# Mixture-of-experts backbone step on one core: the loop over overflow units on TensorE reshaped from two passes of five into one pass and nine, with the counts for unused passes added by VectorE or ScalarE

## The reference, cut to what matters

```python
g_idx = jnp.argmax(g_logits, axis=-1)                 # one of 4 groups
top_v, top_i = lax.top_k(e_logits, TOP_K)             # 2 of the group's 4 experts
top_w = jax.nn.softmax(top_v, axis=-1) * g_w
expert_id = g_idx[:, None] * EXPERTS_PER_GROUP + top_i
combine = jnp.sum(one_hot(expert_id, N_EXPERTS) * top_w[..., None], axis=1)
hidden = silu(einsum('nd,edf->nef', x, w_gate)) * einsum('nd,edf->nef', x, w_up)
y = einsum('nef,efd->nd', hidden * combine[:, :, None], w_down)
```

## Time and profile before

| | |
|---|---|
| time, median of 3 runs | 1340.03 us (1337.36 to 1342.93) |
| span of the profiled execution | 1339.8 us |
| PE busy (matmul) | 1237.9 us, 92% |
| PE weight loads busy | 685.1 us, 51% |
| DVE / ACT / POOL busy | 519.8 / 299.0 / 134.4 us |
| moved from and to device memory | 346.14 MB, mean 258 GB/s |
| granted TensorE clock, mean | 0.984 of full speed |

### The profile page before, as it was taken

The page is one execution under the profiler, slowest core; times in us unless marked ns, Lnnn a source line. Parts: engine busy times, 40 slices in busy tenths (PEclk is TensorE's granted clock), DMA queues, the critical chain, the costliest instruction groups (busy, mean ns, idle before and its releaser), DMA issues. The chain is left out here.

```text
span 1339.8 us, 14616 instructions
## 1 busy us (share of the span) xinstructions
PE 1237.9 (92%) x5692; PEld 685.1 (51%) x5692; DVE 519.8 (39%) x1021; ACT 299.0 (22%) x713; POOL 134.4 (10%) x142
## 2 busy tenths in 40 slices
PE   5999989999998988788999999999999989999897
PEld 2543356445543334244767766776676454453332
DVE  1376666043100002544543646546565561000035
ACT  2123245042111110105121222211223241111112
POOL 0079900000000010001101000000000000000010
PEclk8999999999999999898999999999999999999999
DMA  9859995465999995531232321322234849999995
GB/s 383 338 195 381 373 418 241 187 253 226 403 422 424 426 427 238 247 126 44 99 125 72 141 79 71 134 83 113 83 110 167 378 180 393 424 427 424 426 425 227
DMA packets 35958, 346.14 MB, mean 258 GB/s; under 512 B 3984, under 2 KB 9360, under 8 KB 16528
## 3 DMA queue, kind: packets, MB, share of 16 engines
q1 hardware_dynamic: 23328, 315.37, 57.9%
q0 software_dynamic: 5040, 18.35, 3.4%
q10 hardware_dynamic: 7488, 11.01, 2.3%
HBM read 326.10 MB, written 18.61 MB: 257 GB/s over the span
## 5 line engine op out<-in xcount | busy, mean ns | idle before, releaser
L656 PE MATMUL PS<-ring,hT 128*128 128x512 f32 x432 | 190.5, 595 | 0.0
L872 PE MATMUL PS<-ring,hT 128*64 128x512 f32 x736 | 169.1, 607 | 18.5 <-issue 10.9
L656 PEld LDWEIGHTS PS<-ring,hT 128*128 128x128 f32 x432 | 81.3, 191 | 98.5 <-issue 97.7
L872 PEld LDWEIGHTS PS<-ring,hT 128*64 128x64 f32 x736 | 59.6, 140 | 124.0 <-issue 119.8
L1077 PE MATMUL PS<-ring 128*128 128x256 f32 x480 | 108.7, 379 | 1.2 <-ACT ring L1525 1.2
L1077 PEld LDWEIGHTS PS<-ring 128*128 128x128 f32 x480 | 91.1, 190 | 14.0 <-issue 1.6
L2086 DVE TENSOR_TENSOR area<-area,PS 128x512 f32<-128x512 f32 x16 | 11.0, 688 | 222.0 <-PE PS L872 222.0
L892 PE MATMUL PS<-ring,area 128*64 128x512 f32 x400 | 91.2, 605 | 4.6 <-DMA ring<-moe_w_down 2.4
L1058 PE MATMUL PS<-ring,area 128*128 128x512 f32 x192 | 83.8, 593 | 3.8 <-ACT area L1613 3.8
L1077 PE MATMUL PS<-ring,hT 128*128 128x256 f32 x360 | 82.6, 379 | 0.0
L872 PE MATMUL PS<-area,hT 128*64 128x512 f32 x272 | 69.0, 618 | 12.3 <-issue 12.3
(11 more groups left out here) (308 smaller groups left out, 1507.7 us busy)
## 6 DMA issues: line engine op xcount, KB each, us to landing
ring<-moe_w_down SPq DMA_DIRECT2D x25, 2048.0 KB, 19.4
ring<-mod_w SPq DMA_DIRECT2D x24, 2048.0 KB, 11.3
ring<-moe_w_up SPq DMA_DIRECT2D x24, 2048.0 KB, 14.5
ring<-moe_w_gate SPq DMA_DIRECT2D x22, 2048.0 KB, 14.8
ring<-in_w SPq DMA_DIRECT2D x20, 2048.0 KB, 7.9
area<-moe_w_up SPq DMA_DIRECT2D x8, 2048.0 KB, 15.3
area<-moe_w_gate SPq DMA_DIRECT2D x8, 2048.0 KB, 14.7
ring<-out_w SPq DMA_DIRECT2D x7, 2048.0 KB, 8.8
```

The costliest lines, as they stand in the source:

```text
L656: mm = pe.matmul(out, lhs(k), rhs(k), start=k == 0, stop=k == KD - 1)
L872: mm = pe.matmul(PS[64 * e:64 * e + 64, j, :], gT[:, 4 * half + k, 64 * e:64 * e + 64], w[e][k], start=half == 0 and k == 0, stop=half == ...
```

## The change

On TensorE the loops change from two groups of five to a first pass of one unit and a second pass of nine: the inner loop runs `v * (OVS - 2) + 1` times, which is one for v = 0 and nine for v = 1. The outer `If` has no `Else` any more. Where a pair has exactly one unit, the counts of the nine others are added to `ov_pe` by another engine, ACT for pairs 0 to 5 and DVE for pairs 6 and 7, beside the counts that it adds there already.

```diff
-OVG = 5
...
-                        with pe.Fori(0, OVS // OVG) as v:
-                            with pe.If(n > v * (OVG * OVC) + CAP):
-                                with pe.Fori(0, OVG) as u:
-                                    with pe.If(n > v * (OVG * OVC) + u * OVC + CAP):
-                                        unit(p, v * (OVG * da) + u * da + a, v * (OVG * db) + u * db + b,
-                                             v * (OVG * dc) + u * dc + c, v * OVG + u + e, W)
+                        with pe.Fori(0, 2) as v:
+                            with pe.If(n > v * OVC + CAP):
+                                with pe.Fori(0, v * (OVS - 2) + 1) as u:
+                                    with pe.If(n > v * OVC + u * OVC + CAP):
+                                        unit(p, v * da + u * da + a, v * db + u * db + b, v * dc + u * dc + c, v + u + e, W)
                                     with pe.Else():
-                                        pe.wait_ge(ov_pe, v * (OVG * da) + u * da + a)
+                                        pe.wait_ge(ov_pe, v * da + u * da + a)
                                         pe.sem_inc(ov_pe, da)
                                     pe.nop()
-                            with pe.Else():
-                                pe.wait_ge(ov_pe, v * (OVG * da) + a)
-                                pe.sem_inc(ov_pe, OVG * da)
                             pe.nop()
...
                             act.wait_ge(ov_act, b + db)
                             act.sem_inc(ov_act, db * (OVS - 1))
                             if not direct:
+                                act.sem_inc(ov_pe, da * (OVS - 1))
                                 act.wait_ge(ov_stored, 32 * o + 48)
...
                             dve.wait_ge(ov_dve, c + dc)
                             dve.sem_inc(ov_dve, dc * (OVS - 1))
+                            if direct:
+                                dve.sem_inc(ov_pe, da * (OVS - 1))
                             dve.wait_ge(ov_picks, e + 2)
```

## The result

The changed kernel takes 1333.57 us (median of 5 runs, 1332.43 to 1338.18), the kernel before 1342.93 beside it: ratio 0.994, 95% interval 0.9921 to 0.9958. Run again among the experiments it gave 0.9944 (0.9929 to 0.9959), so some 8 us are gone. The forecast was 1332.7, range 1329.5 to 1338.5. The profiled executions, 1339.8 and 1330.6 us, differ by 9.2.

What follows compares the result with a forecast made beforehand. PE, busy 92% of the span, was taken to bound the kernel, its sequencer walking through empty loop code behind pair 6's unit. 1340.0 - 5.2 - 3.0 + 0.3 + 0.6 = 1332.7 us, range 1329.5 to 1338.5.

Steps and rivals of the forecast that it cites:

- The passes that go: Behind pair 6's unit in layer 0: four skipped passes of 1.17 us go, 4.7 us; with the tail, idle shrinks 5.2 us.
- Where PE starts again: Pair 7's first matmul in layer 0 moves from 547.2 to 542.0, 5.2 us, bounds 5.0 and 5.5.
- The clock: Pair 7's first sixteen matmuls behind the gap no longer run slowly: 3.0 us gained, bounds 0 and 3.0.
- the nearer row: Behind pair 6: 0.3 us idle taken as like the unit's pauses (clock held), not the 2.42 us stop (0.56).
- the clock falls all the same: Rival behind pair 6: sparse matmuls and short gap still lower the clock, only 5.2 us gained, 1335.7; chance 0.12.
- the gap only changes its name: Rival at pair 7's start: another wait or the new arithmetic keeps PE idle some 4 us, 1338 to 1340; chance 0.08.
- Pair 7: Behind pair 7's unit, layer 0: no gain, DVE is last and 5.6 us idle stays; slow spell behind costs 0.3 more.
- DVE in addition: One more semaphore instruction on DVE, 0.1 us with its gap, fits in 0.24 us free: costs nothing.
- Where the code comes to lie: Line 1015's short-way branches: moved code may turn them long or short, 2.3 us each; 0.6 us lost taken.
- The rivals built on the branches: One to three short branches turn long, 1334.4 to 1339.0, chance 0.14; all four, 1341.3 or 1344.3, chance 0.06.

Runs made afterwards that it cites:

- an idle time made in another way: Changed kernel plus 80 (or 24) already satisfied waits before pair 7's gate sweep in layer 0; ratio to the kernel before 0.9971 (24 waits: 0.9943).
- the execution with the 40 waits: Kernel before plus 40 satisfied waits in pair 0's jumped-over overflow code, never executed, so later TensorE code lies 40 instructions further; ratio 0.9996.
- the stop by hand: Kernel before plus 56 satisfied waits in front of pair 5's gate sweep in layer 0; ratio 0.9989.
- the ten skips: Kernel before with one group of ten units instead of two of five (OVG 10), nine skips instead of four; 1348.49 us, ratio 1.0056.
- TensorE adding the counts: Changed kernel's loops, but TensorE adds the nine counts in an outer Else, ScalarE's and VectorE's additions removed; ratio to the kernel before 0.9954.
- the filled gap: Kernel before, skips left, plus six idle-filling matmuls behind pair 6's unit in layer 0; ratio 0.9972.
- all gaps filled: Changed kernel plus six filling matmuls behind pair 7's unit and two ahead of ten short ways; ratio to the kernel before 0.9939.

## Why the prediction was right

**The passes that go** were right, place and size: 5.31 us against 5.2, with no skip left. Five more of them made the idle time 3.9 us longer (4.5 expected), and an idle time made in another way cost its length at the place too. (Of the taken branches in the earlier trace rows one took 176 and one 323 ns, so 215 to 229 does not hold for all; the passes' own were 215 to 226, and the sum stands.)

**Where PE starts again:** the forecast start was 542.0, the trace has 539.44; 2.44 of the difference is the lead that came from before pair 6. The exit compared with a register cost nothing that can be seen: the sequencer is ready 0.2 us behind the unit's end.

**The clock** was right, 2.93 against 3.0, and the choice of the nearer row holds: at this place 0.20, 0.91 and 1.78 us leave it up, 4.61 and 5.51 bring it down. The rival "the clock falls all the same" is out, and so is "the gap only changes its name": nothing else was late. That the size fits so well is in part luck. Behind nearly the same gap the sixteen matmuls lost 2.80 us in the execution with the 40 waits (6.45 against 3.65) and only 1.56 in that with the stop by hand, and behind the 9.38 us of the ten skips 1.39. Between 1.9 and 2.7 us the length of an idle time alone does not tell whether the clock falls. PE's timelines of the stop by hand, of the changed kernel and of TensorE adding the counts:

```profile
546.82 5.21 PE L872 MATMUL PS<-ring,hT 128*64 128x512 f32 x16 [5.46 <-PEq L1040]
```

```profile
484.48 5.35 PE L871 MATMUL PS<-area,hT 128*64 128x512 f32 x16 [1.97 <-issue]
```

```profile
493.53 3.66 PE L871 MATMUL PS<-ring,hT 128*64 128x512 f32 x16 [2.68 <-DMA ring<-moe_w_up]
```

Behind 1.97 us the granted clock was 0.68 (484.4 to 489.8 us), behind 2.68 it was 1.00 (493.5 to 497.1). What decides there is not shown.

**Pair 7** gained nothing, as said; the slow spell behind it has 0.4 us more PE work in it (from 596.29 to 600.87 against 606.98 to 611.16), so 0.2 us lost against 0.3.

**DVE in addition** cost nothing: the semaphore at 541.7 stands in time that DVE had free, for behind its sums DVE still waits 1.34 us for PE.

**Where the code comes to lie** was mis-sized. The step priced a branch that turns long at 2.3 us and took a quarter of one. It also counted ten of the fourteen branches as showing: nine do, and the tenth stop is the one at 1269.63 in the middle of a sweep. One short branch did turn long, and PE stopped 2.63 us, but in layer 0 the price was nothing: the wait for weights absorbs it (the stop in pair 5 shows that). In layer 1 the price of a stop was not shown: the changed kernel stands 11.2 us for "issue" there instead of 14.0, without the stop in the sweep, and takes no less time for it. The rivals built on the branches were wrong in price for layer 0, not only in count.

The Trainium skill ("Runtime: NRT & Kernel Launch", "Instruction fetch mechanics") is borne out in that jumps to far code stop the engine. The same section of the Trainium skill calls the crossing of a fetched block mostly hidden. That agrees with most packets, for of the 70 that queue 8 brings in the kernel before, 55 come without a jump of line 1015 and without a stop for "issue" of over 0.4 us; the stops of 2.87 and 2.13 us in the middle of a sweep, each with a packet landing in it, are not hidden.

Against the sum: 5.3 + 2.9 + 2.4 (pair 6's earlier end) - 0.2 make 10.4, and 9.2 are measured in the traces. The 1.2 between are lost in layer 1, where some spells of low clock and waits moved. In none of the thirteen profiled executions does a unit run in layer 1, and from its first transposes to the end they take from 732.8 us (the kernel before) to 738.5 (ten skips), so a loss of 1 or 2 us there can't be put down to the change. The mechanism was right at the place; that the total came so near is in part luck, since 2.4 us came that were not forecast and 1.2 went. In layer 1's pair 7 PE stops for DVE's product, which stands behind sums that waited for gathered rows; DVE's timeline and PE's wait from 1280 to 1330 us in the changed kernel:

```profile
1301.05 1.28 DVE L2040 SCALAR_TENSOR_TENSOR ring<-ring,area 128x1024 f32<-128x1024 f32 x1 [8.55 <-DMA ring<-yd,idx]
```

```profile
PE PS L880 <- DVE area L2082: 2.5, 1, 2.5
```

What stays open is whether pair 6's earlier end belongs to the change. In the thirteen profiled executions its scatter's start lies between 508.6 and 514.3 us. The five in which pair 4's branch was short (the kernel before, the filled gap, TensorE adding the counts, the 40 shifted waits, all gaps filled) have 511.5 to 514.3; the seven in which it was long 508.6 to 511.5; the one with the stop by hand has 513.3. Among the seven is the kernel with ten skips, which has the old loops, so an early start is not peculiar to the changed ones. The stop by hand shows that stopping there costs nothing; that it brings a gain is not shown, and one execution of each can't settle 2 us. Nor is the rule known by which a branch comes out short or long.

## What to carry to other kernels

Count what a sequencer does when a loop has nothing left to do, and look where the array would start next: a pass of skips is cheap only under cover, and with more passes the cover may not reach (nine instead of four behind pair 7). Price an idle time of a few microseconds with the slow clock behind it, but with a range: behind this gap it was 1.4 to 2.9 us, from one execution to the next. Before a stop is priced, see whether the engine waits for transfers a little later: in layer 0 such a stop was free. And do not take two totals that agree for a proof: follow the lead from one place of the trace to the next.

## What was not expected of the hardware

- TensorE also stops for "issue" in straight code, 2.87 and 2.13 us in the middle of a sweep, and each such stop, like each long jump of line 1015, ends 1.3 to 1.6 us behind the landing of a 16 KB packet of instructions.
- A stop can be paid for by a later wait: PE came to pair 5 4.9 us later, by a stop of 2.71 us and by a slow spell in pair 4, and was 0.3 us earlier at pair 6's scatter, because the waits for weights fell from 4.6 to 0.38 us and a slow spell went.
- The low clock behind the same gap of 5.5 us cost 2.93 us in one execution and 1.56 in another, and behind a gap of 9.4 us 1.39.
- A satisfied wait took TensorE's sequencer 55 to 66 ns: 80 of them lengthened the idle time by 4.41 us, 24 by 1.58.
